# Two prompt units scored ahead of the last value tile, with small products spread between wide ones, in a transformer-layer kernel

## What is computed

```python
def compress(x, pe, w1, w2):
    ...
    for r in range(m):
        proj = jnp.einsum('ncsgd,sdh->ncgh', ch + pe[r][:, None, :], w1[r])
        hsum = hsum + proj[:, r:r + n_cmp]
    return jnp.einsum('ncgh,hd->ncgd', jax.nn.gelu(hsum), w2)
...
def nsa_prompt(qb, kvb, gb, W):
    ...
    kc = compress(kvb[:, :, 0], W['pe_cmp'][0], W['w_cmp1'][0], W['w_cmp2'][0])
    vc = compress(kvb[:, :, 1], W['pe_cmp'][1], W['w_cmp1'][1], W['w_cmp2'][1])
    ...
    o_cmp, imp = compressed_attention(qb, pos, kc, vc, n_sel)
    ...
    o_win, _ = banded_attention(qb, kvb[:, :, 4], kvb[:, :, 5], WIN_B - 1)
    return gate_branches(gb, o_cmp, o_slc, o_win)
```

## Time and profile before

| | |
|---|---|
| median of 3 runs | 1318.1 us (1314.79 to 1319.97) |
| the profiled execution | 1320.84 us, span 1319.1 us |
| TensorE matmul busy | 1278.0 us, 97% of the span |
| TensorE weight loads busy | 994.9 us, 75% |
| VectorE, ScalarE, GpSimd busy | 649.7, 362.6, 161.7 us |
| mean granted TensorE clock | 0.990 |

### The profile page before, as it was taken

The page is one execution under the profiler, slowest core; times in us unless marked ns, Lnnn a source line. Parts: engine busy times, 40 slices in busy tenths (PEclk is TensorE's granted clock), DMA queues, the critical chain, the costliest instruction groups (busy, mean ns, idle before and its releaser), DMA issues.

```text
span 1319.1 us, 18985 instructions
## 1 busy us (share of the span) xinstructions
PE 1278.0 (97%) x6678; PEld 994.9 (75%) x6678; DVE 649.7 (49%) x1482; ACT 362.6 (27%) x727; POOL 161.7 (12%) x380
## 2 busy tenths in 40 slices
PE   7999999999999989999999999899999999999999
PEld 6788656677777765765678888588888888888887
DVE  3776532454443424114014670427877888883321
ACT  4766641344443422212100011522121221210000
POOL 1000000111111153245100020021011010100000
PEclk9999999899999999999999998999999999999999
DMA  5431324422232189999556321012222222222240
GB/s 219 152 139 64 120 98 183 113 65 65 81 90 87 47 289 335 320 295 340 180 219 246 113 79 48 17 64 65 80 82 80 94 80 80 81 104 88 88 151 17
DMA packets 79073, 170.12 MB, mean 129 GB/s; under 512 B 10530, under 2 KB 46307, under 8 KB 78083
## 3 DMA queue, kind: packets, MB, share of 16 engines
q1 hardware_dynamic: 60658, 109.89, 24.8%
q10 hardware_dynamic: 13648, 47.49, 9.7%
q0 software_dynamic: 4672, 11.54, 2.6%
HBM read 159.07 MB, written 9.81 MB: 128 GB/s over the span
## 4 chain that ended last, share of the span: by engine, by line
PE 89%; DVE 4%; issue 3%; ACT 2%; DMA 1%; POOLq 1%; POOL 0%; ACTq 0%; SPq 0%; DVEq 0%
PE ps L2414 18%; PE ps L2451 11%; PE ps L2223 10%; PE ps L1046 9%; PE ps L490 9%; PE ps L1522 7%; PE ps L2256 4%; PE ps L545 3%; PE ps L983 2%; PE ps L969 2%; PE ps L955 2%; PE ps L472 1%; PE ps L493 1%; PE ps L1622 1%; PE ps L1573 1%
## 5 line engine op out<-in xcount | busy, mean ns | idle before, releaser
L2414 PE MATMUL ps<-arena 128*128 128x272 f32 x1120 | 257.1, 392 | 0.5 <-DVE arena L2747 0.5
L2414 PEld LDWEIGHTS ps<-arena 128*128 128x128 f32 x1120 | 212.7, 190 | 44.8 <-DVE arena L2747 1.0
L490 PE MATMUL ps<-arena 128*128 128x272 f32 x512 | 122.9, 399 | 6.8 <-DVE arena L605 6.8
L1046 PE MATMUL ps<-arena 128*128 128x256 f32 x512 | 122.8, 394 | 3.4 <-DVE arena L1153 3.2
L1522 PE MATMUL ps<-arena 128*128 128x272 f32 x512 | 121.1, 395 | 1.7 <-issue 1.1
L2451 PE MATMUL ps<-arena 128*128 128x272 f32 x528 | 121.8, 392 | 0.0
L1046 PEld LDWEIGHTS ps<-arena 128*128 128x128 f32 x512 | 97.5, 195 | 31.2 <-issue 15.0
L490 PEld LDWEIGHTS ps<-arena 128*128 128x128 f32 x512 | 98.9, 194 | 27.5 <-issue 6.8
L1522 PEld LDWEIGHTS ps<-arena 128*128 128x128 f32 x512 | 96.0, 190 | 28.5 <-issue 9.7
L2451 PEld LDWEIGHTS ps<-arena 128*128 128x128 f32 x528 | 100.3, 190 | 20.7
L2223 PE MATMUL ps<-arena 128*128 128x272 f32 (+2 forms) x384 | 90.9, 399 | 0.5 <-DVE arena L2550 0.5
(11 more groups left out here) (363 smaller groups left out, 1688.5 us busy)
## 6 DMA issues: line engine op xcount, KB each, us to landing
arena<-in_w_close SPq DMA_DIRECT2D x68, 512.0 KB, 3.3
arena<-in_pages_cmp SPq DMA_DIRECT2D x128, 128.0 KB, 2.1
arena<-in_past_va ACTq DMA_DIRECT2D x6, 2048.0 KB, 9.6
arena<-in_w_down SPq DMA_DIRECT2D x16, 704.0 KB, 5.8
arena<-in_past_ka ACTq DMA_DIRECT2D x6, 1792.0 KB, 10.7
arena<-in_w_close ACTq DMA_DIRECT2D x16, 512.0 KB, 5.1
arena<-in_w_proj SPq DMA_DIRECT2D x15, 512.0 KB, 3.3
arena<-in_pages_ks SPq DMA_DIRECT2D x80, 64.0 KB, 4.4
```

What stands on the lines that cost most here:

```text
L490: last = pe.matmul(ps[:, 2 * (j % 2) + a, 0:HALF], w, h[:, k, a * HALF:(a + 1) * HALF], start=(k == 0), stop=(k == KD - 1))
L1046: last = pe.matmul(parts(kv)[r], w1[:, kv, r, s1, :], x[:, kv, s1], start=(s1 == 0), stop=(s1 == 7))
L2414: last = pe.matmul(ps[:, bank(f, i), 0:HALF], w[:, k * P:(k + 1) * P], halved[:, rhs, k, :], start=(k == 0), stop=(k == 3))
```

## The change

1. Scores of units 0 and 1 are now issued ahead of value tile 6, the last one; their score rows go into `m.oa`, since the old place is part of the weights that tile 6 still reads. `low`, `total` and `factor` move too.
2. `prompt_project` is cut into eight groups of 4 products. One stands after each second product of value tile 6, the last after the tile.
3. `cmp_scores` is cut into eight groups of 4 products. One stands after each product of piece 2.
4. ScalarE takes value tile 6 between the exponentials of unit 1 and of unit 2; VectorE finishes its gate and scales `h` between `weigh(0)` and `prompt_first`.
5. In `project`, the sum behind the first two memory value tiles comes after 6 products instead of 4, and the sum for the memory no longer waits for the mean before it.

```diff
-        for w in WORK:
+        for w in WORK[:-1]:
             ...
+        m.take_last_values = lambda: values(NVAL - 1)
...
-            if nth(r) > 1:
+            if nth(r) > 1 and r != "mem":
                 pe.wait_ge(v_ready, nth(r) - 1)
...
-                    if k == 4:
+                    if k == 6:
                         sums_between()
...
                         last = pe.matmul(out, h[:, k, t * P:(t + 1) * P], w_val[:, k, cols_],
                                          start=(k == 0), stop=(k == KD - 1))
+                        if fill is not None and (cols_.start, k) != (512, KD - 1):
+                            fill(k + (cols_.start > 0) * KD)
...
+        m.last_values = lambda fill: values(NVAL - 1, fill)
...
+    def score_of(i, e):
+        if i < 2:
+            n = width(i)
+            return m.oa[:, 6 + i, e * n:(e + 1) * n]
+        return score[:, i % 4, e, :]
...
             if t == P_PROJ:
+                m.take_last_values()
                 prompt_second()
...
+        def prompt_project(n):
+            kv, r, half = n // 4, n // 2 % 2, n % 2
+            for s1 in range(4 * half, 4 * half + 4):
+                last = pe.matmul(p_parts(kv)[r], w1[:, kv, r, s1, :], chunked[:, kv, s1, :],
+                                 start=(s1 == 0), stop=(s1 == 7))
+            if n == 7:
+                last.then_inc(proj_full, 1)
...
             for s1 in range(8):
                 last = pe.matmul(parts(kv)[r], w1[:, kv, r, s1, :], x[:, kv, s1], start=(s1 == 0), stop=(s1 == 7))
+                if fill is not None and s1 < 7:
+                    fill(s1)
...
-            if t in (1, 2):
-                pe.wait_ge(m.val_out, m.NVAL - 2 + t)
+            if t == P_PROJ:
+                pe.wait_ge(m.val_out, m.NVAL - 1)
+                pe.wait_ge(w_in, 16 * 4)
+                pe.wait_ge(chunked_ready, 9)
+                m.last_values(lambda k: prompt_project(k // 2) if k % 2 else None)
+                prompt_project(7)
+            if t == 2:
+                pe.wait_ge(m.val_out, m.NVAL)
...
-                piece(n)
+                if t == C_SCORES and n == pieces_before(t):
+                    piece(n, cmp_scores)
+                    cmp_scores(7)
+                else:
+                    piece(n)
...
-        m.finish_values(dve, step)
-        dve.wait_ge(m.gate_ready, QT + 1)
+        m.finish_values(dve, step, [QT] + list(range(QT - 1)))
...
             if t == 1:
+                m.finish_values(dve, step, [QT - 1])
                 m.scale_h(dve, QT - 1)
+                dve.wait_ge(m.gate_ready, QT + 1)
```

More of the change, by code:

```diff
@@ L507, in columns, with values @@
             last.then_inc(col_full, 1)
-        def values(u):
+        def values(u, fill=None):
             def sums_between():
@@ L549, in values @@
             last.then_inc(val_full, 1)
-        for kind, n in WORK:
+        for kind, n in WORK[:-1]:
             product(n) if kind == "tile" else values(n)
@@ L658, in scale_h, with finish_values @@
             .then_inc(m.h_scaled, 1)
-    def finish_values(dve, step):
-        for t in [QT] + list(range(QT)):
+    def finish_values(dve, step, tiles_):
+        for t in tiles_:
             n = SN if t == QT else P
@@ L695, in attend_prompt @@
     kc, c_max, c_sum = at(37752, C), at(37784, QT, 8), at(37816, QT, 8)
-    low, total, factor = at(37848, 4, 2), at(37856, 4, 2), at(37864, 2, 2)
+    low, total, factor = at(43608, 4, 2), at(43616, 4, 2), at(43624, 2, 2)
     chunked = at(37944, 2, 8, 66)
@@ L858, in exps @@
             for e in range(2):
-                last = act.activation(score[:, i % 4, e, 0:n], score[:, i % 4, e, 0:n], ACT.Exp,
+                last = act.activation(score_of(i, e)[:, 0:n], score_of(i, e)[:, 0:n], ACT.Exp,
                                       bias=low[:, i % 4, e:e + 1], scale=-1.0,
@@ L968, in turn @@
                 for k in range(units[i][2] + 1):
-                    last = pe.transpose(ps[:, 4 + e, k * P:(k + 1) * P], score[:, i % 4, e, k * P:(k + 1) * P],
+                    last = pe.transpose(ps[:, 4 + e, k * P:(k + 1) * P], score_of(i, e)[:, k * P:(k + 1) * P],
                                         m.ident[:, :])
@@ L1013, in prompt_small, with cmp_scores @@
             last.then_inc(s_full, 1)
[L1015 to L1025, removed]
+        def cmp_scores(n):
+            if n == 0:
+                s_slot(("cmp", 0))
+                pe.wait_ge(s_act, 1)
+            b, qt = slot_of(("cmp", 0)), n // 2
+            for j in (0, 1) if n % 2 == 0 else (2, 3):
+                for e in range(2):
+                    half = slice(e * HD, (e + 1) * HD)
+                    at = (4 * qt + j) * 32
+                    last = pe.matmul(ps[:, b + e, at:at + C], m.z[half, QB + j, qt * P:(qt + 1) * P],
+                                     kc[half, :], start=True, stop=True)
+            if n == 7:
+                last.then_inc(s_full, 1)
         def cmp_turn():
@@ L1035, in cmp_turn, with piece @@
             last.then_inc(t_full, 1)
-        def piece(n):
+        def piece(n, fill=None):
             s, kv, r = n // 4, n // 2 % 2, n % 2
@@ L1064, in on_pe @@
                 scores(t)
-            if t in (1, 2):
-                pe.wait_ge(m.val_out, m.NVAL - 2 + t)
+            if t == P_PROJ:
[6 more added lines that the diff above has]
+                pe.wait_ge(m.val_out, m.NVAL)
             if t == P_SMALL:
                 prompt_small()
-            if t == C_SCORES:
-                cmp_scores()
             for s in range(NSEQ):
@@ L1081, in on_pe @@
                 values(t - 3)
-            if t == P_PROJ:
-                pe.wait_ge(w_in, 16 * 4)
-                prompt_project()
     def on_dve(dve):
@@ L1098, in evict @@
                 dve.sem_inc(begun, 1)
-                last = dve.tensor_tensor_reduce(score[:, i % 4, e, 0:n], ps[:, b + e, 0:n], mask, -SCALE, 3e38,
+                last = dve.tensor_tensor_reduce(score_of(i, e)[:, 0:n], ps[:, b + e, 0:n], mask, -SCALE, 3e38,
                                                 ALU.add, ALU.min, low[:, i % 4, e:e + 1])
@@ L1114, in weigh @@
             for e in range(2):
-                row = score[:, i % 4, e, 0:n]
+                row = score_of(i, e)[:, 0:n]
                 last = dve.tensor_scalar(row, row, f[:, e:e + 1], None, ALU.mult)
```

## The result

The changed kernel takes 1325.2 us, the median of 5 runs (1324.95 to 1329.16), against 1318.19 us for the kernel before (1314.79 to 1321.0). The ratio of the runs is 1.0042, with a 95% interval of [1.0025, 1.0059]: slower by 5.5 us, inside the 0.5% called no change. The two medians lie 7.0 us apart (1.0053), which is inside the same interval. The forecast was 1323.0 us, and the median is inside its range.

The account below looks back on a forecast made before the run. The prediction took TensorE, busy for 97% of the span, to bound the kernel, through waits, slow products and low clock. Terms summed to +4.9 us, 1325.7 against the profiled execution, so a median of 1323.0 us; range 1315.5 to 1327.5.

Parts of the forecast that it names:

- spreading `prompt_project`: Value tile 6: each of eight switches to small products costs nothing to one load, 0 to 0.9 us, taken as +0.5.
- spreading `cmp_scores`: Piece 2: the wide product's load is exposed at switches, 0.11 us each, 0 to 0.9 us, taken as +0.5.
- end of the last value tile: Turn of unit 1 starts later after T, the end of `prompt_project`, as cover is lost: +1.6 us, bounds 0 and 2.5.
- first fall: Low clock in piece 0, after the last value tile, stays and may last longer: 0 to 1.25 us, taken as +0.6.
- second fall: Low clock in piece 2 goes, as `cmp_scores` alternates with wide products at clock 1.00: -1.7 us.
- VectorE's late chain: `cmp_evict` starts behind piece 2, so idle time ahead of piece 4 grows from 1.77 to 4.3 us: +2.5 us.
- third fall: The longer wait ahead of piece 4 lets the clock fall in piece 4: 0 to 3.65 us, taken as +2.0.
- 1: The clock holds in the wait before piece 4: sum +2.9, 1321.0 us, chance 0.20.
- 2: The clock falls too where piece 2 alternates with `cmp_scores`: sum +8.4, 1326.5 us, chance 0.17.
- 3: The clock never falls after the last value tile: sum -2.6, 1315.5 us, chance 0.08.
- 5: The move of `cmp_scores` doesn't matter, as `add` ahead of piece 4 isn't late: 1318.5 us, chance 0.07.
- 4: Small loads of `prompt_project` and `cmp_scores` hide under wide products: sum -1.4, 1316.7 us, chance 0.06.

Follow-up runs that it names:

- Experiment 3: The kernel before with only `cmp_scores` spread through piece 2: 1325.9 us, ratio 1.0041 to the kernel before.
- experiment 2: The changed kernel with `cmp_scores` put back in one block ahead of piece 2: 1321.23 us, ratio 0.9992 to the kernel before.
- 6: The kernel before with part 5, and `cmp_weigh` one step later on VectorE: 1314.83 us, ratio 0.9954 to the kernel before.
- 7: The changed kernel with `cmp_weigh` one step later on VectorE: 1322.58 us, ratio 1.002 to the kernel before.
- Experiment 4: The changed kernel with VectorE's scaling of `h` for the last tile moved behind `weigh` of unit 2: 1325.72 us, ratio 1.0041 to the kernel before.
- Experiment 5: The changed kernel with spread `cmp_scores` multiplying 128 rows instead of 64, so its results differ: 1325.98 us, ratio 1.0031 to the kernel before.
- early_only: The first experiment: the kernel before with part 5 alone; 1316.77 us, ratio 0.9966 to the kernel before.

## Why the prediction was right, step by step

| step | predicted | measured in the profile, start to start |
|---|---|---|
| memory sum | -0.6 | -0.7 (L472 to L472: 7.86, now 7.14) |
| sum after six products | -0.9 | -1.2 (L472 to L493 behind the sum: 117.71, now 116.51) |
| wait ahead of value tile 6 | +0.4 | +0.5 |
| spreading `prompt_project` | +0.5 | 0 |
| spreading `cmp_scores` | +0.5 | +2.6 (2.4 in the rounds, 0.2 ahead of piece 2) |
| end of the last value tile | +1.6 | +1.3 (T + 5.2, was T + 3.8) |
| first fall | +0.6 | -0.2 (piece 0: 5.88, was 6.10) |
| second fall | -1.7 | -1.7, clock 1.00 |
| VectorE's late chain | +2.5 | +2.4 (13.75 from piece 2's end to piece 4, was 11.37) |
| third fall | +2.0 | +1.7 (5.38, was 3.69) |
| sum | +4.9 | +4.7 |

**Right in mechanism.** Both new waits came where they were put, 2.88 and 3.85 us where 3.2 and 4.3 were written, and the third fall came. Experiment 3 shows that part 3 alone makes a loss as large as the whole, experiment 2 that without it none is left, and 6 and 7 that its chain runs through `cmp_weigh`. Experiment 4 shows VectorE's queue in the turn's wait. What would have shown the sum wrong, waits under 2 us, did not appear. Of the signs of being right, two were missed in size: the wait ahead of the turn is under 3 us, and the alternating stretch took 9.55 us, not some 7.8.

**Wrong in weight.** "This is what I think decides" stood at the end of the last value tile, with 1.6 us. It measured 1.3. Part 3 decides: its terms were +0.5 - 1.7 + 2.5 + 2.0 = +3.3 and measured +2.6 - 1.7 + 2.4 + 1.7 = +5.0.

**Luck in the sum.** The term for `cmp_scores` was 2.1 us too small, and the others together were 2.3 us too large (0.8 of it in the first fall, 0.5 in `prompt_project`). That +4.9 met +4.7 is partly this cancelling.

**Mis-sized: the term for spreading `cmp_scores`.** I counted one exposed load of at most 0.11 us a switch, 0 to 0.9, and took 0.5. Measured from start to start: as blocks, `cmp_scores` takes 3.59 us (257.21 to 260.80) and a piece at full clock 3.56 (251.36 to 254.92), 7.15 together; alternating they take 9.55 (256.47 to 266.02). That is 2.4 us for eight rounds, 0.30 us each for two switches, beyond my upper end. Experiment 5 shows that it goes with weights of unequal rows. The term for `prompt_project`, whose rows are equal, was 0 instead of 0.5.

**Behind the stretch.** The measured column adds to +4.7 us. The kernel before showed the sum ahead of all edits, and piece 5, at:

```profile
31.51 1.08 PE L472 MATMUL ps<-arena 128*128 128x272 f32 x4
...
284.96 3.72 PE L1046 MATMUL ps<-arena 128*128 128x256 f32 x16
```

The changed kernel's execution was 0.7 us early at the first (30.84), which no edit explains, and 4.0 us late at piece 5 (289.00): 4.7 in all. At the end it is 5.5 late. Between lie three things. A fall of the clock at 472 us is missing now (1.6 us back). At 500 us TensorE waits 1.12 us for a transfer of pages, which it did not before (1.4 us with what surrounds it). And behind that wait the clock falls (1.6 us). Windows over both falls, before and after (the work in the same window is shifted by 2 to 6 us), and the wait:

```profile
472.00:477.00 5.00, 4.51 (x28) 0.66 1.02 415
502.00:506.00 4.00, 4.00 (x19) 1.00 1.04 389
```

```profile
472.00:477.00 5.00, 1.94 (x17) 1.00 0.91 297
502.00:506.00 4.00, 4.00 (x32) 0.57 0.96 367
```

```profile
500.08 1.07 PE L1570 MATMUL ps<-arena 128*32 128x512 f32 x8 [1.12 <-DMA arena<-in_pages_ks]
```

No edit touches this code; why the transfer comes later against TensorE there was not tested. "The shift should reach the end" held only as a sum of such pieces.

**Rivals.** 1 fell (the clock did not hold in that wait), 2 fell (1.00 in the mixed stretch), 3 fell, 5 fell (the chain was late by 2.4). 4, small loads hidden under wide products, fell: eight 66-column instructions still take 0.84 us. The Trainium skill (TensorE: Matmul & The Clock Gate, "Step-by-step: what each phase is for") has loads pulled ahead of running products when the row groups do not conflict or the load goes to the background buffer. The trace agrees for the one load behind a product of equal rows (experiment 5) and shows none for 64 rows behind 128. The wide reading in the prediction had left these conditions out.

**Open.** `early_only` gained 4.5 us where its waits explain 1.9. The rest goes with the clock, whose mean was measured in every execution: 0.9914 over the twelve of `early_only`, 0.9890 over the 24 of the kernel before beside it. Among those 24, all of one kernel, the time falls by some 1.2 us for each 0.001 of clock (a fitted line, from 1327.17 us at 0.986 to 1317.32 us at 0.992). The 0.0025 are then some 3 us, an estimate. Why the clock falls in one execution and not in another is not shown: the same code has both.

## What to carry to other kernels

A block of small products is also a cover: before it is spread, ask whose work lies beside it, and when the result that its last product releases is needed. Spreading delays that last product to the end of the wide work. Long steps of a side branch belong behind what the next wide product waits for: moving one `if` by a step took 1.4 us off a wait. A saved low clock is worth little if a new wait makes another. And before a single profile is read, compare its time and its mean clock with those of the other executions: here the profile of `early_only` was its slowest execution.

## What the runs showed of the hardware

- Going from 128-row to 64-row weights and back costs 0.30 us a round (1.19, against 0.89 for the same work in two blocks): the first 64-row load starts 0.33 us after the wide loads end, against 0.03 with equal rows. With 128 rows in both a round takes 1.33 us, only 0.14 more than 1.19.
- A single float32 load of 128 columns lasts 0.19 us with 64 rows and with 128 alike (medians 0.188 and 0.192). In a series they follow each other every 0.057 us with 64 rows, upper and lower half in turn (`cmp_scores`), and every 0.113 us with 128 (`prompt_project`).
- Executions of one kernel differ by their clock: the 24 of the kernel before beside experiments 1 to 4 run from 1317.32 us (mean clock 0.992) to 1327.17 us (0.986).
- In single profiles the same wait of 1.5 us ahead of the turn of unit 2 was followed by a clock of 0.50 for 10.2 us in the kernel before and by none in `early_only`; with the wait of 1.8 us ahead of piece 4 it was the other way round.
